# Layer norms split into two sets of tokens, with shifted sums, chunk waits by quarters, and the next stage's first products interleaved

## The reference

```python
for i in range(DEPTH):                                   # DEPTH = 2
    h = _swiglu(x, ffn1_w_gate[i], ffn1_w_up[i], ffn1_w_down[i])
    x = _layer_norm(ALPHA * x + MACARON_WEIGHT * h, ln_gain[i, 0], ln_bias[i, 0])
    m = _pool_mixer(...) if i % N_MIXERS == 0 else _dilated_attention_mixer(...)
    x = _layer_norm(ALPHA * x + m, ln_gain[i, 1], ln_bias[i, 1])
    h = _swiglu(x, ffn2_w_gate[i], ffn2_w_up[i], ffn2_w_down[i])
    x = _layer_norm(ALPHA * x + MACARON_WEIGHT * h, ln_gain[i, 2], ln_bias[i, 2])
```

## Time and profile before

| | us |
|---|---|
| median of 3 runs | 3693.67 |
| lowest, highest | 3688.31, 3696.8 |
| the profiled execution, device time | 3696.79 |
| its span in the trace | 3695.0 |

### The profile page before, as it was taken

The page is one execution under the profiler, slowest core; times in us unless marked ns, Lnnn a source line. Parts: engine busy times, 40 slices in busy tenths (PEclk is TensorE's granted clock), DMA queues, the critical chain, the costliest instruction groups (busy, mean ns, idle before and its releaser), DMA issues.

```text
span 3695.0 us, 44683 instructions
## 1 busy us (share of the span) xinstructions
PE 3427.4 (93%) x16956; PEld 2730.3 (74%) x16956; DVE 1397.3 (38%) x2017; ACT 794.8 (22%) x1345; POOL 2489.9 (67%) x2220
## 2 busy tenths in 40 slices
PE   7999889999899989999897999969999996999997
PEld 5887666888688858778785888737678774767875
DVE  5551452111311142341535111165656515565642
ACT  1110212110211022231322110031332312232321
POOL 7997675888688857447364788836556774556674
PEclk9999899999899989999998999979999998999999
DMA  6553222322232222112121232212122231222221
GB/s 195 182 180 106 67 80 68 102 88 94 68 102 89 94 80 92 46 58 80 47 80 46 80 93 95 92 56 80 55 66 66 83 97 47 75 58 70 68 90 59
DMA packets 321309, 311.62 MB, mean 84 GB/s; under 512 B 11504, under 2 KB 304016, under 8 KB 320912
## 3 DMA queue, kind: packets, MB, share of 16 engines
q1 hardware_dynamic: 303840, 277.91, 24.2%
q10 hardware_dynamic: 17328, 31.78, 2.6%
HBM read 307.56 MB, written 2.10 MB: 84 GB/s over the span
## 4 chain that ended last, share of the span: by engine, by line
PE 85%; DVE 7%; ACT 5%; issue 2%; POOL 1%; DMA 0%; ACTq 0%; SPq 0%; DVEq 0%; POOLq 0%
PE ps L373 55%; PE ps L1264 15%; PE ps L1024 4%; PE ps L1306 2%; PE ps L478 1%; PE ps L1831 1%; ACT x L509 1%; DVE at_sc L947 1%; ACT xh L515 1%; PE ps L1644 1%; PE ps L1615 1%; DVE x L529 1%; DVE stats L496 1%; DVE at_nb L963 1%; DVE stats L534 1%
## 5 line engine op out<-in xcount | busy, mean ns | idle before, releaser
L344 POOL TENSOR_TENSOR wh<-w_raw,zero 128x512 fp32r<-128x512 f32 (+3 forms) x1108 | 1136.6, 1036 | 1164.3 <-PE ps L373 781.9
L348 POOL TENSOR_TENSOR wl<-w_raw,wh 128x512 fp32r<-128x512 f32 (+3 forms) x1108 | 1410.1, 1283 | 0.0
L373 PE MATMUL ps<-xh,wh 128*128 128x512 f32 x2160 | 858.4, 397 | 96.7 <-DVE xl L551 43.8
L373 PE MATMUL ps<-xl,wh 128*128 128x512 f32 x2160 | 848.1, 393 | 0.0
L373 PE MATMUL ps<-xh,wl 128*128 128x512 f32 x2160 | 847.7, 392 | 0.0
L373 PEld LDWEIGHTS ps<-xh,wh 128*128 128x128 f32 x2160 | 409.4, 190 | 208.9 <-issue 97.3
L373 PEld LDWEIGHTS ps<-xh,wl 128*128 128x128 f32 x2160 | 409.9, 190 | 86.9
L373 PEld LDWEIGHTS ps<-xl,wh 128*128 128x128 f32 x2160 | 410.8, 190 | 83.0 <-issue 1.0
L1264 PE MATMUL ps<-xh,wh 128*128 128x512 f32 x688 | 290.8, 423 | 9.2 <-ACT stats L1406 6.4
L639 DVE TENSOR_TENSOR ps<-sg,ps 128x512 f32<-128x512 f32 x88 | 61.3, 696 | 627.2 <-PE ps L373 627.2
L373 PE MATMUL ps<-hid_h,wh 128*128 128x512 f32 x704 | 280.0, 398 | 2.2 <-DVE mod L1160 2.2
(11 more groups left out here) (287 smaller groups left out, 4723.9 us busy)
## 6 DMA issues: line engine op xcount, KB each, us to landing
w_raw<-in_w_in SPq DMA_DIRECT2D x120, 512.0 KB, 4.0
w_raw<-in_ffn_w_gate SPq DMA_DIRECT2D x88, 512.0 KB, 4.6
w_raw<-in_ffn_w_up SPq DMA_DIRECT2D x88, 512.0 KB, 4.7
w_raw<-in_attn_w_qkv SPq DMA_DIRECT2D x72, 512.0 KB, 4.5
w_raw<-in_ffn_w_down SPq DMA_DIRECT2D x64, 512.0 KB, 3.6
ada_raw<-in_ada_w ACTq DMA_DIRECT2D x24, 512.0 KB, 4.0
stats<-in_ada_w ACTq DMA_DIRECT2D x24, 512.0 KB, 4.0
w_raw<-in_ffn_w_down SPq DMA_DIRECT2D x32, 384.0 KB, 4.1
```

The lines of the kernel that those rows point to most:

```text
L344: done.append(s["w_hi"].up(pool.tensor_tensor(hi[:, parts[q]], raw[:, parts[q]], zero, ALU.subtract)))
L348: return pool.tensor_tensor(lo[:, parts[q]], raw[:, parts[q]], hi[:, parts[q]].bitcast(F32), ALU.subtract)
L373: mm = self.nc.tensor.matmul(out, a[:, slot, w], b(t), start=start and t == order[0] and q == 0, stop=stop and t == order[-1] and q == 2)
```

## The change

- **Two sets of tokens.** Tokens 0 to 255 are set 0, 256 to 511 set 1 (`half`). Everything from the last two output tiles (6 and 7) on is done per set: `pe_last` forms tiles 6 and 7 with matmuls of 256 columns, in the last chunk both tiles of set 0 before those of set 1; then statistics, multiplication, gain, high and low part, for set 0 and then set 1. In the attention stages a set is 64 of the 128 tokens of each residue.
- **Next stage.** `pe_first` does the first two chunks of the next stage by sets: over set 0 chunk 0 with chunk 1 two tiles behind, over set 1 chunk 0 and then chunk 1. The sums of set 1 (`pe_half_sums`) stand in PE's queue after the fourth group of six matmuls of set 0.
- **Shifted sums.** After output tile 3 the mean of tiles 0 to 3 (`pe_shift`) is subtracted from the residual and tiles (DVE, 8 instructions of 512 columns). Then mean (`off`) and mean of squares of the shifted values are both summed at once: DVE adds up tiles 0 to 5 and their squares beforehand, in two sums of 5 additions, and PE adds three parts per set and sum. The variance is the mean of squares less the squared `off`.
- **Root** by ACT on the variance, and reciprocal by DVE into PSUM (`rstd`); the table of the root is loaded ahead by an instruction on one column.
- **Waits by quarters.** `w_lo` rises with every quarter of a chunk, and the first products of a chunk wait for the quarter they need (`arrival`).
- The down product and `pe_out` are no longer loops. The start stage splits x by sets as well.

The diff, cut to its core:

```diff
+HALF = T // 2
+WHOLE = KT - 2
+TAIL = KT + 2
+NORM = dict(zsum_ready=1, mean_ready=1, shifted=KT, tail_mm=2, sq_ready=TAIL, sums_ready=2, off_ready=2, off_squared=2, var_part=2, var_ready=2,
+            roots=2, std_ready=2, centred=2 * KT, t_ready=2 * KT, x_ready=2 * KT, xh_ready=2 * KT, acts=2 * KT)
...
-            sp.wait_ge(self.s["w_lo"].sem, c + 1)
+            sp.wait_ge(self.s["w_lo"].sem, 4 * c + 4)
...
-                return pool.tensor_tensor(lo[:, parts[q]], raw[:, parts[q]], hi[:, parts[q]].bitcast(F32), ALU.subtract)
+                s["w_lo"].up(pool.tensor_tensor(lo[:, parts[q]], raw[:, parts[q]], hi[:, parts[q]].bitcast(F32), ALU.subtract))
...
-    def wait_chunk(self, pe, c):
-        pe.wait_ge(self.s["w_lo"].sem, PRIMED["w_lo"] + c + 1)
+    def wait_chunk(self, pe, c, quarter=3):
+        pe.wait_ge(self.s["w_lo"].sem, PRIMED["w_lo"] + 4 * c + quarter + 1)
+
+    def arrival(self, pe, c, k):
+
+        quarter = lambda t: -(-4 * (t + 1) // k) - 1
+
+        def before(t):
+            if t == 0 or quarter(t) > quarter(t - 1):
+                self.wait_chunk(pe, c, quarter(t))
+        return before
 
...
+        return self.ps[:, self.VAR_BANK[h], 0:HALF]
+
+    def rstd(self, h):
+        return self.ps[:, self.VAR_BANK[h], HALF:T]
...
+    def pe_shift(self, pe, st):
+
+        s = self.s
+        pe.wait_ge(s["zsum_ready"].sem, st.at("zsum_ready", 1))
+        s["mean_ready"].up(self.nc.tensor.matmul(self.ps[:, self.shift_bank(st)], self.ones[:], self.zsum[:], start=True, stop=True))
+
+    def pe_half_sums(self, pe, st, h, parts=(0, 1, 2)):
+
+        s = self.s
+        for what in range(2):
+            out, signal = ((self.off(h), "off_ready"), (self.var(h), "var_part"))[what]
+            for n in parts:
+                if n == 0:
+                    pe.wait_ge(s["sums_ready"].sem, st.at("sums_ready", what + 1))
+                    part = self.half((self.zsum, self.std)[what], h)
+                else:
+                    name = ("z_ready", "sq_ready")[what]
+                    pe.wait_ge(s[name].sem, st.at(name, WHOLE + 2 * h + n))
+                    part = self.tail_square(n - 1, h) if what else self.half(self.x[:, WHOLE + n - 1], h)
+                mm = self.nc.tensor.matmul(out, self.ones[:], part, start=n == 0, stop=n == 2)
+            if n == 2:
+                s[signal].up(mm)
+
+    LAG = 2
+
+    def pe_first(self, pe, st, residue=False):
+
+        s, c = self.s, st.chunk0
+        before = self.stages[self.stages.index(st) - 1]
+        for h in range(2):
+            for step in range(2 * KT):
+                for n in range(2):
+                    k = step - (self.LAG, KT)[h] * n
+                    if not 0 <= k < KT:
+                        continue
+                    if n == 0:
+                        pe.wait_ge(s["acts"].sem, st.at("acts", KT * h + k + 1 - 2 * KT))
+                    if (h, n, k) == (0, 1, 0):
+                        pe.wait_ge(s["z_ready"].sem, st.at("z_ready", 0))
+                    if h == 0 and k % 2 == 0:
+                        self.wait_chunk(pe, c + n, k // 2)
+                    xh, xl = (self.half(a[:, k], h, residue) for a in (self.xh, self.xl))
+                    for m in range(2):
+                        out = self.half(self.ps[:, 2 * n + m], h, residue)
+                        w = slice(k * 256 + m * P, k * 256 + m * P + P)
+                        for q, (a, b) in enumerate(((self.wh, xh), (self.wh, xl), (self.wl, xh))):
+                            mm = self.nc.tensor.matmul(out, a[:, (c + n) % 2, w], b, start=k == 0 and q == 0, stop=k == KT - 1 and q == 2)
+                        if h == 1 and k == KT - 1:
+                            s["acc"].up(mm)
...
+    def pe_last(self, pe, st, chunks, xs, residue=False):
+
+        s = self.s
+        xh, xl = xs
+        at = 0
+        for n, (c, k, ready) in enumerate(chunks):
+            last = n == len(chunks) - 1
+            self.wait_chunk(pe, c)
+            if ready:
+                ready()
+            for m, h in (((0, 0), (1, 0), (0, 1), (1, 1)) if last else ((0, 0), (0, 1), (1, 0), (1, 1))):
+                if n == 0 and (m, h) == (0, 0):
+                    pe.wait_ge(s["z_ready"].sem, st.at("z_ready", 4))
+                out = self.tail_out(h, m, residue)
+                for t in range(k):
+                    if last and t == 3 and m != h:
+                        self.pe_half_sums(pe, st, 0, (2,) if h else (0, 1))
+                    w = slice(t * 256 + m * P, t * 256 + m * P + P)
+                    for q, (a, b) in enumerate(((self.wh, xh), (self.wh, xl), (self.wl, xh))):
+                        mm = self.nc.tensor.matmul(out, a[:, c % 2, w], self.half(b(at + t), h, residue),
+                                                   start=n == 0 and t == 0 and q == 0, stop=last and t == k - 1 and q == 2)
+                if last and h == 0:
+                    s["tail_mm"].up(mm)
+                if h == 1:
+                    s["acc"].up(mm)
+            at += k
+
...
+    def dve_norm_sums(self, dve, st, ev, out_done, residue=False):
 
         nc, s = self.nc, self.s
-        for m in range(KT):
+        for m in range(4):
             ev(m)
             if m:
                 dve.wait_ge(s["z_ready"].sem, st.at("z_ready", m + 1))
-                a = self.x[:, 0] if m == 1 else self.zsum[:]
...
-
+        dve.wait_ge(s["mean_ready"].sem, st.at("mean_ready", 1))
+        mean = self.ps[:, self.shift_bank(st)]
+        for n, m in enumerate((4, 5, 6, 7, 0, 1, 2, 3)):
+            s["shifted"].up(nc.vector.scalar_tensor_tensor(self.x[:, m], mean, -2 / self.residual(st) if m >= 4 else -2.0, self.x[:, m], ALU.mult, ALU.add))
+        total, squared = {}, {}
+
+        def sums(out, src, m, last, memo):
+            if m > 1:
+                dve.wait_ge(s["dve_step"].sem, memo["t"])
+            ins = nc.vector.tensor_tensor(out, src(0) if m == 1 else out, src(m), ALU.add)
+            if last:
+                s["sums_ready"].up(ins)
+            else:
+                memo["t"] = s["dve_step"].up(ins)
+        for m in range(WHOLE):
+            if m >= 4:
+                if m == 4:
+                    dve.wait_ge(s["shifted"].sem, st.at("shifted", 4))
+                ev(m)
+                dve.wait_ge(s["z_ready"].sem, st.at("z_ready", m + 1))
+            else:
+                dve.wait_ge(s["shifted"].sem, st.at("shifted", 4 + m + 1))
+            if m:
+                sums(self.zsum[:], lambda m: self.x[:, m], m, m == WHOLE - 1, total)
+        for m in range(WHOLE):
+            dve.wait_ge(s["sq_ready"].sem, st.at("sq_ready", m + 1))
+            if m:
+                sums(self.std[:], lambda m: self.squares[:, m], m, m == WHOLE - 1, squared)
+        self.dve_norm(dve, st, lambda m, h: self.dve_tail(dve, st, m, h, out_done, residue))
+
+    def dve_tail(self, dve, st, m, h, out_done, residue):
+        s = self.s
+        if h == 0:
+            dve.wait_ge(s["tail_mm"].sem, st.at("tail_mm", m + 1))
+        else:
+            dve.wait_ge(s["acc"].sem, out_done(m))
+        x = self.half(self.x[:, WHOLE + m], h)
+        if residue:
+            x = self.by_residue(x)
+        s["z_ready"].up(self.nc.vector.scalar_tensor_tensor(x, x, self.residual(st), self.tail_out(h, m, residue), ALU.mult, ALU.add))
 
...
+        def square_off(h):
+            act.wait_ge(s["off_ready"].sem, st.at("off_ready", h + 1))
+            s["off_squared"].up(nc.scalar.activation(self.half(self.zsum, h), self.off(h), ACT.Square))
+
+        def rstd(h, step):
+            v = self.half(self.zsum, h)
+            if step == 0:
+                act.wait_ge(s["var_ready"].sem, st.at("var_ready", h + 1))
+                s["roots"].up(nc.scalar.activation(v, v, ACT.Sqrt, bias=self.eps[:, eps:eps + 1]))
+
+        def tile(m, h):
+            act.wait_ge(s["t_ready"].sem, st.at("t_ready", KT * h + m + 1))
+            x = self.half(self.x[:, m], h)
+            t = s["x_ready"].up(nc.scalar.activation(x, x, ACT.Identity, scale=self.ln[:, 0, u, m:m + 1], bias=self.ln[:, 1, u, m:m + 1]))
+            if self.splits(st.kind, st.index):
+                act.wait_ge(s["x_ready"].sem, t)
+                hi, full, _ = self.split_views(st, m, h)
+                s["xh_ready"].up(nc.scalar.activation(hi, full, ACT.Copy))
+        for m in range(WHOLE):
+            square(m)
+        self.act_then(act, nc.scalar.activation(self.eps[:, 5:6], self.ones[:, 0:1], ACT.Sqrt))
+        square(0, 0)
+        square(1, 0)
+        square_off(0)
+        for step in range(2):
+            rstd(0, step)
         for m in range(KT):
-            act.wait_ge(s["t_ready"].sem, st.at("t_ready", m + 1))
-            t = s["x_ready"].up(nc.scalar.activation(self.x[:, m], self.x[:, m], ACT.Identity,
-                                                     scale=self.ln[:, 0, u, m:m + 1], bias=self.ln[:, 1, u, m:m + 1]))
-            if not self.splits(st.kind, st.index):
```

(108 more changed lines are left out.)

206 lines of the change are left out of this document (110 added, 96 removed).

## The result

| | before | after |
|---|---|---|
| median, us (4 runs each, taken side by side) | 3690.99 | 3664.39 |
| lowest, highest | 3688.0, 3696.8 | 3662.01, 3666.47 |
| ratio of the times, 95% interval | | 0.9926 [0.9909, 0.9943] |
| profiled execution, its span | 3696.79, 3695.0 | 3666.47, 3664.6 |

The forecast was 3654 in a range of 3630 to 3684; the time is inside it, and 10 us above the forecast.

A forecast was written before the change was run, and what follows sets the result against it. PE was taken to bound the kernel, norms mattering where it stands still. Gains 9.4 + 9.3 + 11.3 + 3.8 + 3.2 + 4.8 - 2.5 = 39.3 us off 3696.8 give 3657.5; the runs' median lies 3.1 lower: 3654, range 3630 to 3684.

The forecast's parts named there:

- The bound and the yardstick: PE sets the end; a norm's loss is its stretch's time over the 22.2 us that 96 products need.
- The feed-forward end: Norm after ffn 0 and 1: loss 17.5 us against 26.9 and 26.8, gain 9.4 and 9.3; PE idles 3.0.
- six more subtractions 7.0: DVE's set 0 chain at a feed-forward end: six offset subtractions after the reciprocal (4.95), done at 7.0 us.
- new work: PE's 12 half sums and mean of tiles 0 to 3, now in line with products: 6.3 us per feed-forward norm.
- The clock's term, 1.7: After each feed-forward restart, half speed for 3 to 10 us costs 0.5 to 4 us; 1.7 taken.
- POOL and DVE in each other's way: POOL splitting during a norm slows DVE's low parts: 3 us per feed-forward end, middle taken (15.8 between 14.3 and 17.3).
- The ends of pool and attention: DVE's work ahead of the sums doesn't fit: 5.7 us over a feed-forward end, losses 23.2 and 24.2, gain 3.8 and 3.2.
- POOL's lead, "I cost that at 0": POOL gets chunk 2's slot 5.8 us ahead of PE's need, and waits ask for one quarter then: cost 0.
- The start: PE starts sooner but its fourth group waits for chunk 1's first quarter, at 30.5: cost +2.5 us (0 to +5).
- Ffn 3: Last norm, without low parts or following products: 19.4 us against 24.2, gain 4.8.
- the clock doesn't stay down: Rival: `pe_first`, fed tile by tile, leaves the clock low in five norms; 31.7 us slower, 3725 us, chance 0.06.
- the sets do overlap: Rival: a new wait holds PE until set 1 is ready, restart 15 us later in five norms; 3729 us, chance 0.04.

The follow-up runs named there:

- run 9: Changed kernel with DVE scaling tile 0 of the first token set before centring tiles 2 to 7: 3651.90 us, 12.5 us less.
- run 11: run 10's kernel plus unread matmuls in both waits, 14 ahead of tile 0 and five behind its products: 3632.98 us, 2.9 us less than run 10.
- run 5: Changed kernel with DVE's running sums at the pool and attention ends kept in PSUM: 3653.41 us, 11.0 us less.
- run 3: Changed kernel with POOL splitting only a quarter of each part of three pool-stage chunks, the rest left out: 3658.69 us, 5.7 us less.
- run 1: Changed kernel without its waits by quarters, products waiting for whole chunks: 3710.55 us, ratio to before 1.0044.
- runs 6: Changed kernel with the pool and attention shift taken from tiles 0 and 1, and additions of squares between those of tiles: 3645.49 us, 18.9 us less.
- run 10: Changed kernel with pool and attention shift from two tiles, their running sums in PSUM, and group weights waited for by quarters: 3635.84 us.

## Why the prediction was right, and where it wasn't

**The bound and the yardstick.** PE sets the end and a norm matters where PE stands still: right. The table above has the gain where the sum had it, in ffn 0, 1 and 2, with 31.0 us for 30.0.

**The feed-forward end.** The idle time before the restart is 3.75, 3.68 and 3.86 us for 3.0. The steps up to "six more subtractions 7.0" are there (2.06 us for the six), and run 9 shows that they needn't stand in it; what was short is the low part, 1.31 us at 412.23 for the 0.42 in that sum and the 0.77 allowed beside POOL. The 0.77 was read wrong: in the trace of before it is a mean of 0.42 with POOL idle (2788.40) and 1.02 to 1.51 beside it (3533.90, 2784.34), and not the price beside POOL. The tiles then come with one wait of 0.84 to 1.43 us for 1.4. Set 1 waits nothing in ffn 1 and some 2.6 us in ffn 2 (1.07 and seven of 0.22) for 2. The twelve half sums took 4.9 us in ffn 0 (1.54 for the four at 400.71, 0.68 for two at 404.92, 2.72 for six at 420.01) and 5.6 in ffn 1, the mean of tiles 0 to 3 0.45, each counted to the next product's start. The product behind that one comes late as well (0.30 us instead of 0.12 after each group of half sums, 0.63 instead of 0.23 after the mean), and with that the new work in ffn 0 is 5.5 + 0.85, the 6.3 of the forecast. The clock's term, 1.7, is near what run 11 took back (1.5, 1.8 and 1.0). The errors have both signs and cancel to 1 us over three norms: the mechanism was right, that the sum came so near is in part luck.

**POOL and DVE in each other's way** was put at +3 per end, of which half went into the sum. In the feed-forward ends it shows in the first low parts alone (0.92 to 1.49 us with POOL at work until 419.7, 0.42 later with POOL idle). In pool and attention an addition took 1.51 us for 0.70 (run 5), where the 1.17 of the earlier trace rows had been my upper bound. The page GPSIMD Engine Reference of the Trainium skill (Specifications), by which DVE's instructions with two SBUF inputs contend with POOL, has the place right: one operand moved to PSUM ended it.

**The ends of pool and attention** are the term that was mis-sized. The row of shifts, additions and squares was laid out rightly, down to PE standing at its first sum for "4 to 10 us"; PE's waits were 9.0 and 9.4, the upper end. Against a feed-forward end I had put 5.7 and 6.7 us on top, and it came to 8.7 and 11.5 (losses of 26.0 and 28.8 for the 17.3 of ffn 0 and 1). A low clock is a part of that: at pool the granted clock is 0.51 in the last 4.6 us of the wait already, and the matmuls start 0.21 us apart for 5.7 us behind it, to 550.3, where the first feed-forward end has 6.8. Gain +1.0 and -1.4 instead of +3.8 and +3.2: the sum was 7.4 us too high by them.

**POOL's lead, "I cost that at 0".** This step failed, in the pool stage. A slot comes free 5.4 us ahead of PE's need (439.45 for 444.89), as worked out, and the quarters cover that; but three chunks in a row, two of them at 11 us and more, leave nothing over, PE waits 5.0 us for POOL, and 6.3 us are lost (run 3). The forecast named it among the things that would prove it wrong, yet gave it no price; that the time still fell in the range is owed to its width, not to this step. In the feed-forward stages POOL catches up and nothing is lost. And the cover that made it 0 elsewhere, the quarters, hid 46 us (run 1): without them the kernel is slower than before, and the forecast doesn't say that its gain hangs on them.

**The start** was put at -2.5 and came out at +0.3: POOL had the second chunk's first quarter split at 27.5 and not 30.5 (it began 0.6 us sooner, at 13.49, and its parts took 1.22 and 1.45 us for 1.49 and 1.72), and PE's matmuls start every 0.12 us again from 31.6 on, 4 us after the restart.

**Ffn 3** gained 5.9 for 4.8. The rivals: the clock doesn't stay down (0.90 to 0.95 in the five stretches, not 0.50), the sets do overlap. Summing the errors: +2.8 at the start, +1.0 in the feed-forward ends, +1.1 at ffn 3, -2.8 and -4.6 at the ends of pool and attention, -6.3 inside pool, make 8.8 us less than the 39.3 forecast, 30.5, which is the 30.4 by the spans.

## What to carry to other kernels

A restructuring that takes idle time out of the busiest engine also takes it from whoever worked in its shadow: before counting the gain, follow the next engine's buffers through the shortened stretch, and hand over in smaller parts where its lead shrinks (run 1: 46 us, against 27 for the whole change). In a chain that hands tiles over one by one, do for tile 0 what tile 0 needs and nothing else, and put statistics that have a choice of sample on the earliest tiles (runs 6 and 9: 18.9 and 12.5 us, each by a few moved lines).

## What was not expected of the hardware

POOL pays for the meeting in SBUF, too: beside DVE's additions from two SBUF operands (1.51 us) its own instructions took 1.50 and 1.71 us; with one of DVE's operands in PSUM (0.70) they took 1.04 and 1.40. The granted clock fell to 0.50 behind a wait of 1.43 us that followed six matmuls, with only 0.62 us idle before them, and stayed at 1.00 when that wait was filled with matmuls that nobody reads. The length of the wait alone doesn't tell, though: in run 10 PE waited 2.46 us at the end of pool and the clock stayed at 1.00, while behind 2.45 us at the end of attention it was down. What parts the two stays open.
